# The decay levels of a chunked linear recurrence: seven levels in four visits, or a block-of-four step and five levels in two

## What is computed

```python
def step(state, inp):
    qc, kc, vc, gc = inp
    bcum = jnp.cumsum(gc, axis=2)
    diff = bcum[:, :, :, None, :] - bcum[:, :, None, :, :]
    decay = jnp.where(causal, jnp.exp(jnp.where(causal, diff, 0.0)), 0.0)
    attn = jnp.sum(qc[:, :, :, None, :] * kc[:, :, None, :, :] * decay, axis=-1)
    o = (jnp.einsum('bhts,bhse->bhte', attn, vc)
         + jnp.einsum('bhtd,bhde->bhte', qc * jnp.exp(bcum), state))
    blast = bcum[:, :, -1:, :]
    new_state = (jnp.exp(blast)[:, :, 0, :, None] * state
                 + jnp.einsum('bhsd,bhse->bhde', kc * jnp.exp(blast - bcum), vc))
    return new_state, o
```

## Time and profile before

| | |
|---|---|
| median of three runs | 1025.34 us |
| the profiled execution's own time | 1027.41 us |
| its span, first to last instruction | 1025.6 us |
| mean granted clock of PE | 0.997 |
| PE busy | 1013.7 us (99%) |
| DVE busy | 642.7 us (63%) |
| ACT busy | 517.2 us (50%) |
| POOL busy | 287.4 us (28%) |
| the chain that ended last | PE 92%, DVE 5%, ACT 1%, issue 1%, DMA 1% |

### The profile page before, as it was taken

One profiled execution on the slowest core, in us unless ns is written; L12 is line 12 of the kernel. 1 busy time (PEld: TensorE's weight loads), 2 busy tenths in 40 slices (PEclk: granted clock), 3 DMA queues, 4 the chain that ended last, 5 costly groups with the idle time before them and its releaser, 6 DMA issues.

```text
span 1025.6 us, 15346 instructions
## 1 busy us (share of the span) xinstructions
PE 1013.7 (99%) x6406; PEld 855.2 (83%) x6406; DVE 642.7 (63%) x840; ACT 517.2 (50%) x804; POOL 287.4 (28%) x144
## 2 busy tenths in 40 slices
PE   8999999999999999999999999999999999999997
PEld 7878999788888888888888989988888888888876
DVE  6978965899444443536638689479973444444552
ACT  6866665865633222323366766567546323232333
POOL 1122114324332323324112111153243232322430
PEclk9999999999999999999999999999999999999999
DMA  7532122122232323325243222212232232322602
GB/s 222 153 103 64 63 83 83 42 83 83 62 103 83 103 82 103 99 68 162 83 134 103 67 79 84 83 49 77 83 103 62 82 103 84 101 89 96 204 2 82
DMA packets 93428, 94.71 MB, mean 92 GB/s; under 512 B 2272, under 2 KB 91568, under 8 KB 93360
## 3 DMA queue, kind: packets, MB, share of 16 engines
q1 hardware_dynamic: 93232, 93.70, 29.8%
q10 hardware_dynamic: 128, 0.04, 0.0%
HBM read 91.64 MB, written 2.10 MB: 91 GB/s over the span
## 4 chain that ended last, share of the span: by engine, by line
PE 92%; DVE 5%; ACT 1%; issue 1%; DMA 1%; SPq 0%; DVEq 0%; ACTq 0%
PE pj L512 27%; PE pj L513 26%; PE pj L514 26%; PE mx L649 2%; PE mx L512 1%; PE mx L513 1%; PE mx L514 1%; PE mx L612 1%; PE mx L709 1%; PE mx L677 1%; PE mx L597 1%; PE mx L687 1%; PE mx L589 1%; DMA x_tokens<-in_x 1%; DVE rope_cos L1427 1%
## 5 line engine op out<-in xcount | busy, mean ns | idle before, releaser
L1168 POOL TENSOR_TENSOR w_lo<-w_raw,w_hi 128x1024 fp32r<-128x1024 f32 (+1 forms) x89 | 195.9, 2201 | 566.5 <-ACT w_hi L825 566.3
L512 PE MATMUL pj<-h_hi,w_hi 128*128 128x512 f32 x832 | 329.7, 396 | 0.4 <-DVE w_lo L1278 0.4
L514 PE MATMUL pj<-h_hi,w_lo 128*128 128x512 f32 x832 | 324.2, 390 | 0.0
L513 PE MATMUL pj<-h_lo,w_hi 128*128 128x512 f32 x832 | 324.1, 389 | 0.0
L825 ACT ACTIVATE w_hi<-w_raw 128x1024 fp32r<-128x1024 f32 (+1 forms) x179 | 159.1, 938 | 160.3 <-PE pj L514 160.1
L1278 DVE TENSOR_TENSOR w_lo<-w_raw,w_hi 128x1024 fp32r<-128x1024 f32 (+1 forms) x90 | 159.9, 1777 | 67.9 <-ACT w_hi L825 67.7
L512 PEld LDWEIGHTS pj<-h_hi,w_hi 128*128 128x128 f32 x832 | 156.2, 188 | 34.8 <-issue 3.2
L514 PEld LDWEIGHTS pj<-h_hi,w_lo 128*128 128x128 f32 x832 | 156.2, 188 | 33.1
L513 PEld LDWEIGHTS pj<-h_lo,w_hi 128*128 128x128 f32 x832 | 156.3, 188 | 31.9 <-issue 1.0
L1392 DVE TENSOR_TENSOR merge_gate<-pj,rstd 128x512 f32<-128x512 f32 x48 | 33.2, 692 | 162.9 <-PE pj L514 162.9
L943 ACT ACTIVATE merge_gate<-merge_gate,small 128x512 f32<-128x512 f32 x48 | 34.3, 715 | 89.3 <-DVE merge_gate L1392 89.3
(11 more groups left out here) (259 smaller groups left out, 1502.0 us busy)
## 6 DMA issues: line engine op xcount, KB each, us to landing
w_raw<-in_w_in SPq DMA_DIRECT2D x61, 1024.0 KB, 5.5
w_raw<-in_w_branch SPq DMA_DIRECT2D x24, 512.0 KB, 3.4
w_raw<-in_w_out SPq DMA_DIRECT2D x6, 1024.0 KB, 5.2
x_tokens<-in_x SPq DMA_DIRECT2D x4, 512.0 KB, 7.3
w_raw_last<-in_w_out SPq DMA_DIRECT2D x2, 1024.0 KB, 8.1
sp_w_rows<-in_sp_w SPq DMA_DIRECT2D x2, 512.0 KB, 6.3
out<-out_low SPq DMA_DIRECT2D x4, 256.0 KB, 2.0
out<-out_high SPq DMA_DIRECT2D x4, 256.0 KB, 2.3
```

The lines of the kernel that those rows point to most:

```text
L512: pe.matmul(bank, wh, ah, start=first, stop=False)
L513: pe.matmul(bank, wh, al, start=False, stop=False)
L514: return pe.matmul(bank, wl, ah, start=False, stop=final)
L1168: return pool.tensor_tensor(out=dst, in0=full, in1=hi.bitcast(f32), op=ALU.subtract)
```

## The change

The diagonal and the levels of 2 and 1 tokens (levels 5 and 6) become one step on blocks of four tokens: keys and queries of each block are multiplied by the decay from or to the point between its second and third token, one set of 32 matmuls takes the place of the diagonal's, and a mask copies the lower triangle of each 4x4 block. `block4_diffs` makes twice the distance from that point in one DVE operation over 128x1024, after an addition over 128x256; ACT takes two exponentials of it, with scales 0.5 and -0.5; `block4_operands` multiplies keys and queries, 128x1024 each. Levels 0 and 1 are now read by PE together with this step, after job d+1, and levels 2, 3 and 4 together after job d+4, with d = 12 or 26 (was 25). Levels 0 and 1 lie in the halves of bank `mx3`, 2 and 3 in those of `mx4`, 4 again in `mx3`. The last steps (`transpose_khat` and after) come at d+9 for the first pair, job 21 as before, and at d+7 for the second, job 33 instead of 34.

```diff
-LEVELS = 7
-DIAG = (12, 25)
-PAIRS = ((0,), (1, 2), (3, 4), (5, 6))
+LEVELS = 5
+DIAG = (12, 26)
+LATE = (9, 7)
+MASKS = 16 + 8 * (LEVELS - 1)
+VISITS = ((0, 1), (2, 3, 4))
...
+        HK = [at(f"key_blocks{p}", [P, 2 * T], r) for p, r in enumerate((r_brh + 16 * KB, r_brl + 8 * KB))]
+        HQ = [at(f"query_blocks{p}", [P, 2 * T], r) for p, r in enumerate((r_sg, r_scr + 12 * KB))]
...
+        def level_ops(p, lev):
+            return HK[p] if lev == LEVELS - 1 else XL[lev % 2]
+
+        def level_bank(lev):
+
+            return (M[3][:, 0:T // 2], M[3][:, T // 2:T], M[4][:, 0:T // 2], M[4][:, T // 2:T], M[3][:, 0:T // 2])[lev]
...
                 def diagonal(p):
-                    evacuated(pe, FIRST[("cq", p)] + 1, layer)
-                    pe.wait_ge(c_keys, upto(c_keys, p + 1))
+                    pe.wait_ge(ops_ready, upto(ops_ready, (LEVELS + 1) * p + 1))
                     if p == 1:
                         pe.wait_ge(oc_rstd, upto(oc_rstd, 1))
                     for hb in range(2 * TB):
-                        hh, tb = divmod(hb, TB)
                         for half in range(2):
                             rows = slice(half * 64, half * 64 + 64)
-                            b = slice(tb * P + half * 64, tb * P + half * 64 + 64)
-                            last = pe.matmul(M[4][rows, hb * 64:(hb + 1) * 64], KK[p][:, hh, b], QC[p][:, hh, b],
+                            b = slice(hb * P + half * 64, hb * P + half * 64 + 64)
+                            last = pe.matmul(M[4][rows, hb * 64:(hb + 1) * 64], HK[p][:, b], HQ[p][:, b],
                                              start=True, stop=True)
...
-                    pe.wait_ge(at_evac, upto(at_evac, (LEVELS + 1) * p + lev))
+                    if lev >= 2:
+                        pe.wait_ge(at_evac, upto(at_evac, (LEVELS + 1) * p + (3 if lev == 4 else 1)))
...
                     hooks[d + 1].append((diagonal, p))
-                    for i, levels in enumerate(PAIRS):
+                    for i, levels in enumerate(VISITS):
                         for lev in levels:
-                            hooks[d + 1 + 2 * i].append((level, p, lev))
+                            hooks[d + 1 + 3 * i].append((level, p, lev))
                     for step, f in enumerate((transpose_khat, state_updates, recurrent_out, head_norm)):
-                        hooks[d + 2 + LEVELS + step].append((f, p))
+                        hooks[d + LATE[p] + step].append((f, p))
...
+                def block4_exp(p):
+                    act.wait_ge(diff_done, upto(diff_done, (LEVELS + 2) * p + 1))
+                    act.activation(E[1][:, :], E[0][:, :], ACT.Exp, scale=0.5)
+                    act.activation(E[0][:, :], E[0][:, :], ACT.Exp, scale=-0.5).then_inc(decay_ready, 1)
...
-                    for i, levels in enumerate(PAIRS):
-                        for lev in levels:
-                            phase[d - 1 + max(lev if i < 2 else 2 * i, 0)].append((decay_exp, p, lev))
+                    phase[d - 2].append((block4_exp, p))
+                    for lev in range(LEVELS):
+                        phase[d + (-1, -1, 0, 0, 3)[lev]].append((decay_exp, p, lev))
...
+                        pool.wait_ge(lev_done, upto(lev_done, 2 * (LEVELS + 1)))
...
+                def block4_diffs(p):
+
+                    if p == 0:
+                        dve.wait_ge(rope_done, upto(rope_done, 5))
+                    else:
+                        dve.wait_ge(state_ready, upto(state_ready, 1))
+                    b = BC[p][:, :, :].rearrange("p h t -> p (h t)").rearrange("p (b u) -> p b u", u=4)
+                    mid2 = E[1][:, 0:2 * T // 4]
+                    chained(dve.tensor_tensor(out=mid2, in0=b[:, :, 1], in1=b[:, :, 2], op=ALU.add))
+                    dve.scalar_tensor_tensor(out=E[0][:, :].rearrange("p (b u) -> p b u", u=4), in0=b, scalar=2.0,
+                                             in1=mid2.unsqueeze(2).to_broadcast([P, 2 * T // 4, 4]),
+                                             op0=ALU.mult, op1=ALU.subtract).then_inc(diff_done, 1)
+
+                def block4_operands(p):
+                    dve.wait_ge(decay_ready, upto(decay_ready, (LEVELS + 2) * p + 1))
+                    if p == 1:
+                        dve.wait_ge(oc_done, upto(oc_done, 1))
+                    dve.tensor_tensor(out=HK[p][:, :], in0=KK[p][:, :, :].rearrange("p h t -> p (h t)"),
+                                      in1=E[0][:, :], op=ALU.mult)
+                    evacuated(dve, FIRST[("cq", p)] + 1, layer)
+                    dve.tensor_tensor(out=HQ[p][:, :], in0=QC[p][:, :, :].rearrange("p h t -> p (h t)"),
+                                      in1=E[1][:, :], op=ALU.mult).then_inc(ops_ready, 1)
...
+                    dve.wait_ge(ops_ready, upto(ops_ready, (LEVELS + 1) * p + max(lev, 1)))
...
+                    back = (0, 0, 2, 3, 1)[lev]
+                    if p + back > 0:
+                        dve.wait_ge(lev_done, upto(lev_done, (LEVELS + 1) * p + back))
...
-                    dve.memset(at4[64:128, :, 0:64], 0.0)
+                    chained(dve.memset(AT[:, :, :], 0.0))
                     for half in range(2):
                         rows = slice(half * 64, half * 64 + 64)
-                        last = dve.tensor_tensor(out=at4[rows, :, half * 64:half * 64 + 64],
-                                                 in0=M[4][rows, :].rearrange("p (b t) -> p b t", t=64),
-                                                 in1=ID[rows, rows].unsqueeze(1).to_broadcast([64, 2 * TB, 64]),
-                                                 op=ALU.mult)
+                        last = dve.copy_predicated(at4[rows, :, half * 64:half * 64 + 64],
+                                                   MASK4[rows, :].unsqueeze(1).to_broadcast([64, 2 * TB, 64]),
+                                                   M[4][rows, :].rearrange("p (b t) -> p b t", t=64))
...
-                    phase[d - 1].append((diffs, p, 0))
-                    phase[d].append((diffs, p, 1))
-                    phase[d].append((operands, p, 0))
-                    phase[d + 1].append((operands, p, 1))
-                    phase[d + 1].append((diffs, p, 2))
-                    phase[d + 2].append((take_diagonal, p))
-                    phase[d + 2].append((take_level, p, 0))
-                    phase[d + 2].append((operands, p, 2))
-                    for i in (1, 2):
-                        for lev in PAIRS[i + 1]:
-                            phase[d + 1 + 2 * i].append((diffs, p, lev))
-                        for lev in PAIRS[i]:
-                            phase[d + 2 + 2 * i].append((take_level, p, lev))
-                        for lev in PAIRS[i + 1]:
-                            phase[d + 2 + 2 * i].append((operands, p, lev))
-                    phase[d + LEVELS].append((block_diffs, p))
-                    for lev in PAIRS[3]:
-                        phase[d + LEVELS + 1].append((take_level, p, lev))
-                    phase[d + LEVELS + 1].append((decayed, p))
-                    phase[d + LEVELS + 4].append((states, p))
-                    phase[d + LEVELS + 6].append((head_scaled, p))
+                    phase[d - 2].append((block4_diffs, p))
+                    phase[d - 1].append((block4_operands, p))
+                    for lev in (0, 1):
+                        phase[d - 1].append((diffs, p, lev))
+                    for lev in (0, 1):
+                        phase[d].append((operands, p, lev))
+                    for lev in (2, 3):
+                        phase[d].append((diffs, p, lev))
+                    phase[d + 2].append((take_block4, p))
+                    for lev in (0, 1):
+                        phase[d + 2].append((take_level, p, lev))
+                    for lev in (2, 3):
+                        phase[d + 3].append((operands, p, lev))
+                    phase[d + 3].append((diffs, p, 4))
+                    phase[d + 4].append((operands, p, 4))
+                    for lev in (2, 3, 4):
+                        phase[d + 5].append((take_level, p, lev))
+                    phase[d + 5].append((block_diffs, p))
+                    phase[d + 6].append((decayed, p))
+                    phase[d + LATE[p] + 2].append((states, p))
+                    phase[d + LATE[p] + 4].append((head_scaled, p))
```

More of the change, by code:

```diff
@@ L79, in constants @@
 def constants():
-    c = np.zeros((P, P + 8 * LEVELS + 8), np.float32)
-    masks = c[:, P:P + 8 * LEVELS].view(np.uint8)
+    c = np.zeros((P, P + MASKS + 8), np.float32)
+    masks = c[:, P:P + MASKS].view(np.uint8)
     c[:, 0:P] = np.eye(P)
+    for i in range(P):
+        for t in range(i % 64, i % 64 // 4 * 4 + 4):
+            masks[i, t] = 1
     for lev in range(1, LEVELS):
@@ L88, in constants @@
             if i % (2 * s) < s:
-                b = i % 64 // (2 * s)
-                masks[i, 32 * lev + b * s:32 * lev + (b + 1) * s] = 1
-    o = P + 8 * LEVELS
```

(20 more changed lines are left out.)

40 lines of the change are left out of this document (12 added, 28 removed).

## The result

The changed kernel took 1029.32 us in the median of five executions (1026.56 to 1030.41), the kernel before 1025.34. The ratio is 1.0033 with a 95% interval of 1.0022 to 1.0044. The forecast was 1022.6 us with a range to 1027.8: wrong in its sign, and the time lies outside the range.

The account below looks back on a forecast made before the run. PE, busy 99% of the span, was taken as the bound: -9.2 us of PE work plus waits of 0.4, 2.9, 0.6 and 2.6 gave -2.7 us, from 1025.34 to 1022.6 us, range 1017.8 to 1027.8.

Parts of the forecast that it names:

- What leaves PE: PE's stream loses two levels in two pairs and layers, 8.0 us, and six own visits, 1.2 us: 9.2 us less.
- Wait (a): First pair, first layer: PE waits at the transposes for the probabilities, which DVE's added scaling and differences delay: 0.4 us.
- Wait (b): First layer, `attend` after job 13: PE waits for ACT's `probsT` copy behind the exponentials, DVE meeting POOL once: 2.9 us.
- Wait (c): Second layer, `attend`: the same wait for ACT's copy, shortened by DVE's 1.09 us to spare: 0.6 us, bounds 0 and 3.1.
- Wait (d): Second pair, job 28: PE waits for DVE's later `w_lo`, 1.3 us in each layer, 2.6 us together.
- rivals' conditions: What each alternative needed: DVE keeps up (chance 0.18), nothing measurable (0.28), or slower through more POOL operations (0.15).
- DVE did not keep up: Denies the first alternative: POOL's splits fall between DVE's operations, leaving 1.4 us of waits, 1017.5 us; chance 0.18.
- each new wait on it is paid in full: Opening step: PE's stream is the time, so work leaving it is gained in full and added waits cost their length.
- a cost left out: Closing remark on signs: a granted clock that falls after one of PE's waits was not counted; no size given.
- Late work makes PE late, and its order leaves DVE no choice: Argument given for the slower alternative, 1032.2 us; against it stood that a late PE moves the next deadline back.
- the third rival: Slower: DVE's queue is one POOL operation longer at four critical places, 9.6 us on top, 1032.2 us; chance 0.15.
- The cover taken for granted: Clearing `attnT`, mask copies, level 4's operations, POOL's new wait and later emptying of banks were costed at nothing.

Follow-up runs that it names:

- e3_both_later: Changed kernel with exponentials of levels 2 and 3 behind the probabilities' copy in both pairs, second pair's differences of these levels one phase later: 1016.26 us, ratio 0.9910.

## Why the prediction was wrong, step by step

**What leaves PE: right, and a little small.** Taken from `e3_both_later`, whose waits are few, PE's stream shrinks by 5.2 us in each layer, 10.4 in all against 9.2 forecast. In a layer the levels and visits of the first pair give 2.35 us (forecast 2.2) and those of the second 2.54 (2.4); a visit of its own that goes with its two levels gives 2.18 to 2.20, as forecast. The moved last steps of the second pair, which the sum left out, give 0.3 us a layer.

**Wait (a), transposes:** 0.4 forecast, 0.51 measured; the addition and the scaling held DVE for 1.79 us (80.41 to 82.20) where 1.6 was laid out, because the addition took 0.6 and not 0.35. **Wait (b), `attend` in the first layer:** 2.9 and 3.11. Its mechanism is the one forecast, link by link: the scaling took 1.2 us as forecast, the third product met POOL and took 2.89 us, and from the end of level 3's differences (99.31) to the end of the copy (101.38) ACT took 2.07 us for the last exponential and the copy (1.1 + 1.07). **Wait (c), the same in the second layer:** 0.6 and 1.11; here too the third product took 2.88 us. **Wait (d), job 28:** 1.3 and 1.84, in each layer; DVE met POOL for as long as before, where the forecast took 0.3 us off. Together 6.5 us forecast and 8.4 measured. None of the rivals' conditions came: DVE did not keep up, and no further POOL operation met it.

**What failed is the step "each new wait on it is paid in full", taken as paid once and no more.** The forecast waits came, by the forecast mechanism, and were 1.9 us longer in all; they alone would still have left a gain of 2.0 us (-10.4 + 8.4). Three things come on top. First, PE resumes late: 8.4 us of waits and the stop raised the distances by about 0.9 us more than their rows say. Second, the stop of 1.70 us (1.3 to 1.8 in three traces) inside level 1. The prediction moved level 1 as 1.00 us of work wherever it stands, and not as 32 rows more in a burst behind a wait. In the trace of its fastest execution, then: -10.4 + 8.4 + 1.7 + 0.9 = +0.6 us where -2.7 was forecast. Its time, 1026.56, is 1.2 us above the median of before; the other 0.6 us lie ahead of the fourth product or around the span, and I have not settled them. Third, the falls of the clock: 2.8 us from the fastest execution to the median, about two stretches of 3.4 us at 1.2 GHz at the 1.3 to 1.6 us that the traces show for one; the median execution itself was not traced. The prediction named such a fall as a cost left out, and neither gave it a price nor let the range hold it. With 2.8 us for it and 1.7 for the stop the same sum would have been 1027.1 us.

**"Late work makes PE late, and its order leaves DVE no choice"**, said for the third rival, was right as an argument, but its mechanism (POOL four times more) was not what made the kernel slower. The range was too narrow because it varied the length of the waits, not what a wait brings with it.

**The cover taken for granted** held: PE waited for no operand of a level, for no bank, and POOL's new wait cost nothing that shows.

## What to carry to other kernels

When PE is the bound, a gain of PE time is bought with the deadlines of the engines that feed it: look which of their operations merely stand ahead of a needed one and move those behind it. Two such edits, of one line each, turned +0.33% into -0.9%. Price a wait of PE at more than its length: here 1.3 us cost up to 1.4, and waits of 1.8 us and more brought, some of the times, falls of the clock at 1.3 to 1.6 us each. Before lengthening a burst of small matmuls, look in the DMA view where its packets of instructions fall, and whether a wait ahead of it pushes one behind a large transfer. Distances between the starts of the same instruction in two traces give the price of each edit to 0.1 us. Executions whose time goes up as the mean granted clock goes down point at stretches of half clock; whether these lie behind waits or in the prologue only a trace tells.

## What the runs showed of the hardware

- The granted clock fell 0.2 to 1.6 us after the end of waits of PE of 1.84, 2.06 and 3.1 us, for 3.4 us each time (five falls in four traces). Not at every one: the fastest execution of the changed kernel has four waits or stops of 1.7 to 3.1 us and no fall. Behind holds of 1.3 us the traced execution has none, and the mean clocks of the eight others (0.998 and 0.999) give no sign of one.
- PE stopped for 1.3 to 2.1 us inside a burst of 156 rows of small products when it had waited 1.1 to 1.5 us ahead of it, after 142 or 146 of them (five stops in four traces). Behind 3.1 us it did not stop in any of three traces, with the same burst. A packet of 16 KB on the queue of instructions lands 1.2 to 1.6 us before each stop ends, and it starts as a weight transfer of 1 MB runs out. PE's instructions arriving late behind that transfer fits all five stops and the three bursts without one; a run that moves the transfer would have to show it, and why the packet does not start while PE still waits stays open.
